# The second MLP product of two token groups as seven block products, with sums of weight and hidden blocks on GpSimd

## The chip, the cores and the metric

One core of one Trainium2 chip. The metric is the device time of one launch in microseconds (us), median of several runs.

## The reference, cut to what matters

One step of a two-layer network over 1152 tokens (128 context tokens and 1024 latent tokens), width 1024, everything in float32. Each layer has a mixer (a short convolution with windowed attention in layer 0, gated linear attention, GLA, in layer 1) and then an MLP with 4096 hidden columns:

```
def sq_relu_mlp(h, w1, w2):
    return jnp.square(jax.nn.relu(h @ w1)) @ w2
...
    x = x + gt1 * rms_norm(mix, norm_g[1])
    h = rms_norm(x, norm_g[2]) * (1 + sc2) + sh2
    x = x + gt2 * rms_norm(sq_relu_mlp(h, w1, w2), norm_g[3])
```

The change is in the last product of that MLP, `(hidden) @ w2`, for 768 of the 1152 tokens, in both layers.

## The kernel before, in words

The 1152 tokens are nine tiles of 128, in three groups of three (`GROUPS`, `GT`; a group is `GN` = 384 tokens). Every float32 product is made as three products of rounded parts: an operand x is split into x_hi, which ScalarE (ACT) writes by a copy to the rounded type, and x_lo = x - x_hi, which VectorE (DVE) writes. The product is hi*hi + hi*lo + lo*hi, three matmuls of TensorE (PE).

The MLP of a layer has three stages on PE.

1. **Group 0**, `mlp_step` and PE's `up` and `down`: for each of 32 hidden rows f the first product (L2545), and with the row before it the second product into the accumulators `acc(0)` to `acc(2)` (L2467), two PSUM banks each, one for every tile of tokens.
2. **Pairs**, `pairs` and PE's `pair_products` (L2580): the first product of groups 1 and 2, for 16 jobs j of two hidden rows each (`JOBS`). A 2x2 block product (two hidden rows by two halves of the inner dimension, times two halves by two groups) is made as seven block products with sums (`PRODUCTS` = 7). A block product is one step: 12 matmuls of 384 columns; a job is 84. DVE makes the weight sums (`sum_weights`, L1925) and the lo parts (`split_piece`, L1932) of job j+1 while PE works at job j, and adds the products (`sum_block`, L1948); its order is written out by hand: step 0 has three weight sums and a split, step 1 has `sum_block` 0 and a split, and so on. PE's step 3 waits for `sum_block` 0, which empties the bank that step 3 writes. ACT applies the ReLU (`relu_block`, L1257), GpSimd (POOL) squares each of the four blocks of a job in place (`square_blocks`, L902), and SyncE (SP) stores them in `hid_scratch` in HBM (`block_out`).
3. **Held rows**: the second product of groups 1 and 2. For group 1 and then group 2 it runs over 32 hidden rows. A row n needs a panel of `mlp_w2` (128x1024, 512 KB) and a stored hidden block (128x384). SP loads both when PE has used the row four before it (`down` and `held_in`, L582 and L720; four slots), ACT rounds both (`round_held`, L1262 and L983), DVE splits both (`split_held`, L1953 and L1601), two rows ahead of PE in their programs, and PE's `rows_panel` (L2467) does 18 matmuls of 512 columns: three tiles, three parts, two halves. After each group `post_square` (ACT) and `post_add` (DVE) read the accumulators, scale them by the norm and add them to `xt`; the first read by DVE frees an accumulator for PE.

Each engine runs its own program in order; semaphores tie them. After layer 0's MLP the first panels of the GLA projection follow (L2649); after layer 1's the output rows are written.

## Time and profile before

| | us |
|---|---|
| median of 3 runs (2780.16 to 2782.31) | 2782.21 |
| the profiled execution, whole | 2780.66 |
| its span, first to last instruction | 2778.9 |
| held rows of layer 1, within the span | 2504.6 to 2768 |
| pairs of layer 0, steady part | 885 to 1098 |

The profile is of one execution. A busy share is busy time over the span. Matmuls overlap in the pipeline, so the time of one is better read from a long run of them divided by their number than from the duration in its row. The time of an instruction of DVE, ACT or POOL runs from when the engine took it up to its end, so it holds any time in which the instruction could not get at its operands.

### The profile page before, as it was taken

How to read it: one execution, taken by the hardware profiler on the slowest of the kernel's cores; microseconds unless marked ns; L12 is line 12 of the kernel's file. 1: busy time of each engine (PE TensorE's matmuls, PEld its weight loads, DVE VectorE, ACT ScalarE, POOL GpSimd, SP SyncE). 2: the span in 40 equal slices, each digit the busy share in tenths (PEclk: the TensorE clock that was granted, in tenths of full speed). 3: DMA queues.
4: the chain of work that ended last, by engine and by line, in shares of the span. 5: the costliest groups of instructions: out<-in, count | busy, mean ns of one | idle time of the engine just before them, and what ended most of it. 6: DMA issues, size and time to landing. Idle time of an engine off the chain costs nothing.

```text
span 2778.9 us, 37923 instructions
## 1 busy us (share of the span) xinstructions
PE 2675.1 (96%) x14835; PEld 2351.4 (85%) x14835; DVE 1608.3 (58%) x2516; ACT 1285.3 (46%) x2216; POOL 312.8 (11%) x308
## 2 busy tenths in 40 slices
PE   5999999999999999999999998889999999999998
PEld 3878888889998999878898886777899989998787
DVE  4246666564567775555522458985645577764444
ACT  5134445554444444444423676764544444443433
POOL 0000000000001222000000007971000002220000
PEclk8999999999999999999999999999999999999999
DMA  7743332633333444554413451025334434436554
GB/s 274 213 152 96 98 98 70 190 119 124 121 122 121 121 127 165 172 192 169 145 46 102 144 167 53 1 70 200 118 121 122 123 113 125 130 124 205 177 191 146
DMA packets 238909, 372.86 MB, mean 134 GB/s; under 512 B 24806, under 2 KB 181932, under 8 KB 237708
## 3 DMA queue, kind: packets, MB, share of 16 engines
q1 hardware_dynamic: 232496, 352.71, 40.0%
q10 hardware_dynamic: 4220, 9.86, 1.0%
q0 software_dynamic: 2016, 7.86, 0.7%
q8 instruction: 119, 1.95, 0.3%
q14 instruction: 58, 0.48, 0.1%
HBM read 329.88 MB, written 40.50 MB: 133 GB/s over the span
## 4 chain that ended last, share of the span: by engine, by line
PE 86%; DVE 5%; ACT 4%; DMA 2%; issue 2%; SPq 1%; POOL 0%; DVEq 0%; ACTq 0%; POOLq 0%
PE ps L2467 39%; PE ps L2580 16%; PE ps L2545 9%; PE ps L2281 8%; PE ps L2649 4%; PE ps L2242 3%; PE ps L2335 2%; PE ps L2362 1%; PE ps L2298 1%; DVE t_g L1790 1%; PE ps L2745 1%; ACT prT L1072 1%; SPq L622 1%; DVE xx L2105 1%; ACT junk_n L1139 1%
## 5 line engine op out<-in xcount | busy, mean ns | idle before, releaser
L1601 DVE TENSOR_TENSOR p_lo<-p_raw,p_hi 128x1024 fp32r<-128x1024 f32 x379 | 465.6, 1231 | 378.9 <-ACT p_hi L983 378.1
L983 ACT ACTIVATE p_hi<-p_raw 128x1024 fp32r<-128x1024 f32 x379 | 397.4, 1051 | 232.4 <-DMA p_raw<-mlp_w 121.7
L902 POOL TENSOR_TENSOR c_out<-c_out 128x384 f32<-128x384 f32 x128 | 117.9, 932 | 1601.7 <-ACT c_out L1257 1601.7
L2467 PE MATMUL ps<-p_hi,hq_hi 128*128 128x512 f32 x768 | 238.7, 392 | 4.8 <-DVE t_g L1790 4.8
L2467 PE MATMUL ps<-p_hi,hq_lo 128*128 128x512 f32 x768 | 236.7, 389 | 0.0
L2467 PE MATMUL ps<-p_lo,hq_hi 128*128 128x512 f32 x768 | 236.6, 389 | 0.0
L1262 ACT ACTIVATE hq_hi<-hq_raw 128x384 fp32r<-128x384 f32 x128 | 67.0, 523 | 268.9 <-DMA hq_raw<-hid_scratch 268.7
L2580 PE MATMUL ps<-t_hi,w_hi 128*128 128x384 f32 x512 | 173.2, 338 | 10.8 <-DVE t_g L1790 7.6
L1953 DVE TENSOR_TENSOR hq_lo<-hq_raw,hq_hi 128x384 fp32r<-128x384 f32 x128 | 71.9, 562 | 187.6 <-ACT hq_hi L1262 187.5
L2580 PE MATMUL ps<-t_lo,w_hi 128*128 128x384 f32 x512 | 172.9, 338 | 0.0
L2580 PE MATMUL ps<-t_hi,w_lo 128*128 128x384 f32 x512 | 172.9, 338 | 0.0
L2467 PEld LDWEIGHTS ps<-p_hi,hq_hi 128*128 128x128 f32 x768 | 142.5, 188 | 35.5 <-DVE t_g L1790 5.6
L2545 PE MATMUL ps<-hm_hi,p_lo 128*128 128x384 f32 x512 | 172.0, 336 | 0.0
L2545 PE MATMUL ps<-hm_hi,p_hi 128*128 128x384 f32 x512 | 171.7, 335 | 0.0
L2545 PE MATMUL ps<-hm_lo,p_hi 128*128 128x384 f32 x512 | 171.5, 335 | 0.0
L2467 PEld LDWEIGHTS ps<-p_lo,hq_hi 128*128 128x128 f32 x768 | 144.2, 188 | 30.3
L2467 PEld LDWEIGHTS ps<-p_hi,hq_lo 128*128 128x128 f32 x768 | 144.2, 188 | 30.1
L2281 PE MATMUL ps<-h_hi,p_hi 128*128 128x384 f32 x432 | 158.8, 368 | 3.9 <-DVE h_lo L1622 3.9
L2281 PE MATMUL ps<-h_hi,p_lo 128*128 128x384 f32 x432 | 145.6, 337 | 0.0
L2281 PE MATMUL ps<-h_lo,p_hi 128*128 128x384 f32 x432 | 145.2, 336 | 0.0
L1932 DVE TENSOR_TENSOR w_lo<-w_pair,w_hi 128x512 fp32r<-128x512 f32 x128 | 104.6, 820 | 49.9 <-ACT w_hi L1236 49.9
L1948 DVE TENSOR_TENSOR c_sum<-ps,c_sum 128x384 f32<-128x384 f32 x160 | 88.8, 555 | 75.3 <-PE ps L2580 71.9
(298 smaller groups left out, 6050.0 us busy)
## 6 DMA issues: line engine op xcount, KB each, us to landing
p_raw<-mlp_w SPq DMA_DIRECT2D x256, 512.0 KB, 3.4
mod_p<-mod_w SPq DMA_DIRECT2D x80, 512.0 KB, 4.2
w_pair<-mlp_w SPq DMA_DIRECT2D x32, 1024.0 KB, 5.8
p_raw<-gla_w_in SPq DMA_DIRECT2D x56, 512.0 KB, 3.6
hid_scratch<-c_out SPq DMA_DIRECT2D x128, 192.0 KB, 1.9
hq_raw<-hid_scratch SPq DMA_DIRECT2D x128, 192.0 KB, 3.4
p_raw<-gla_w_out SPq DMA_DIRECT2D x24, 512.0 KB, 3.4
mod_w<-mod_w SPq DMA_DIRECT2D x8, 1024.0 KB, 19.0
```

Of the source, the lines that this page charges most:

```text
L902: nc.gpsimd.tensor_tensor(c_out[n % 4][:], c_out[n % 4][:], c_out[n % 4][:], ALU.mult).then_inc(c_squared, 1)
L983: nc.scalar.activation(p_hi[s][:, :, 0:width], p_raw[s][:, :, 0:width], ACT.Copy).then_inc(pan_hi, 1)
L1601: V.tensor_tensor(p_lo[s][:, :, 0:width], p_raw[s][:, :, 0:width], p_hi[s][:, :, 0:width].bitcast(F32), ALU.subtract).then_inc(pan_lo, 1)
L1932: V.tensor_tensor(w_lo[layer][i][:], raw_piece(j, step), w_hi[layer][i][:].bitcast(F32), ALU.subtract).then_inc(piece_lo, 1)
L1948: V.tensor_tensor(out[:], b, x[:], ALU.add).then_inc(c_summed, 1)
L1953: V.tensor_tensor(hq_lo[layer][n % 4][:], hq_raw[layer][n % 4][:], hq_hi[layer][n % 4][:].bitcast(F32), ALU.subtract).then_inc(hq_ready, 1)
L2242: return M.transpose(out, in_, ident[0:n, 0:n])
L2281: mm = M.matmul(ps[:, b, 0:GN], w[s][:, c, :], h0[n][x][:, c, :], start=(c == 0 and x == 0 and w is p_hi), stop=(c == DC - 1 and w is p_lo))
L2467: mm = M.matmul(acc(slot)[:, cols], x, flat(w[s])[:, cols], start=begin and edge == 0, stop=end and edge == 2)
L2545: mm = M.matmul(ps[:, b, 0:GN], w[s][:, c, :], x[:, c, :], start=(c == 0 and x is hi and w is p_hi), stop=(c == DC - 1 and w is p_lo))
L2580: mm = M.matmul(ps[:, c_bank(j, which), 0:GN], w[layer][i][:, c, :], second_operand(layer, step, x, c), start=(step < 3 and c == 0 and x = ...
L2649: mm = M.matmul(ps[0:width, b, 0:GN], w[s][:, c, 0:width], hx[g][x][:, c, :], start=(c == 0 and x == 0 and w is p_hi), stop=(c == DC - 1 a ...
```

## The change

The second product of groups 1 and 2 is now also made as seven block products. For each of 16 panel pairs j, the hidden blocks (two groups by two hidden rows) times the weight blocks (two hidden rows by two halves of 512 output columns) are one 2x2 block product. The seven go in four passes, each over all 16 pairs: passes 0, 1 and 3 have two block products for each panel, one in each half of the accumulators (18 matmuls), and pass 2 has one (9 matmuls). So a layer has 64 panels as before, 16 of them with half the matmuls.

- The four sums of hidden blocks (`s1`, `q11`, `s2`, `s4`) are made by POOL after the squares, in `square_blocks`, and seven blocks of a job are stored in place of four (`blocks_out`, `STORED`).
- The sums of weight blocks are made by POOL in `panel_sums`, on 128x512 each: one in pass 0, two in pass 1, one in pass 2. The first is kept in `w_hold` for the later passes. ACT's rounding of such a panel waits for POOL (`pan_summed`).
- Loads of a panel: 512 KB in passes 0, 1 and 3 (in pass 1 as two halves of two panels), 256 KB in pass 2. Loads of hidden blocks: two blocks (384 KB) in passes 0, 1 and 3, one in pass 2.
- Between passes the accumulators are read out: ACT copies them to `pp` after pass 0; DVE makes `second_sums` and `second_rest` after pass 1, `third_sum` after pass 2 (which completes group 1 in `xn`), and `fourth_sum` after pass 3 (which completes group 2 in `pp`). `post_square` and `post_add` of groups 1 and 2 then read `xn` and `pp` in SBUF, no longer PSUM.

The diff, cut to its core:

```diff
+    w_hold = [[at(f"w_hold{l}{j}", [P, CC, P], F32, o + 2048 * j if j < 12 else rest + 2048 * (j - 12)) for j in range(JOBS)]
+              for l, o, rest in ((0, RC, RA + TAIL), (1, RA, RC))]
+    pp = [at(f"pp{l}", [P, GT, D], F32, o + TAIL) for l, o in ((0, RD), (1, RB))]
+    u_sum = at("u_sum", [P, GT, D // 2], F32, RS)
...
+        STORED = ((c_out[1], 5, 1, 2), (c_out[2], 4, 2, 3), (None, 1, 3, 4), (c_out[3], 0, 3, 5), (c_out[0], 3, 0, 6),
+                  (None, 2, 3, 7), (None, 6, 3, 8))
...
+        def held_halves(n):
+
+            return (0, 1) if n // JOBS != 2 else (0,)
+
+        def raw_half(layer, s, n, half):
+
+            kind, j = divmod(n, JOBS)
+            if kind + half == 1 and kind < 2:
+                return w_hold[layer][j][:]
+            return p_raw[s][:, CC * half:CC * (half + 1), :]
...
+                def blocks_out(j):
+
+                    for i, (x, r, k, made) in enumerate(STORED):
+                        if x is None:
+                            x = s_out[layer][{1: 0, 2: 1, 6: 2}[r]]
+                        sp.wait_ge(c_squared, 8 * (JOBS * layer + j) + made)
+                        sp.dma_start(hid_d[j, r], x[:]).then_inc(hid_out[k], 16)
+
+                def rows_in(n):
+
+                    kind, j = divmod(n, JOBS)
+                    s = fed[0] % SLOTS
+                    fed[0] += 1
+                    sp.wait_ge(pan_used, T.next(pan_used))
+                    if kind in (0, 3):
+                        sp.dma_start(p_raw[s][:], w2[2 * j + kind // 3]).then_inc(pan_in[s], 16)
+                    elif kind == 1:
+                        sp.dma_start(p_raw[s][:, 0:CC], w2[2 * j + 1][:, CC:DC]).then_inc(pan_in[s], 16)
+                        sp.dma_start(p_raw[s][:, CC:DC], w2[2 * j][:, CC:DC]).then_inc(pan_in[s], 16)
+                    else:
+                        sp.dma_start(p_raw[s][:, 0:CC], w2[2 * j + 1][:, 0:CC]).then_inc(pan_in[s], 16)
...
+            def panel_sums(layer, n):
+
+                kind, j = divmod(n, JOBS)
+                s, value = panel_landed[layer, n]
+                last_job = PRODUCTS * (JOBS * layer + JOBS - 1)
+                raw = [p_raw[s][:, CC * h:CC * (h + 1), :] for h in range(2)]
+                hold = w_hold[layer][j][:]
+                if n == 0:
+                    pool.wait_ge(product, last_job + 1)
+                    pool.wait_ge(piece_lo, last_job + PRODUCTS)
+                if n == 3:
+                    pool.wait_ge(product, last_job + PRODUCTS)
+                    pool.wait_ge(c_relu, 4 * JOBS * (layer + 1))
+                pool.wait_ge(pan_in[s], value)
+                if kind == 0:
+                    nc.gpsimd.tensor_tensor(hold, raw[1], raw[0], ALU.subtract).then_inc(pan_summed, 1)
+                elif kind == 1:
+                    nc.gpsimd.tensor_tensor(hold, raw[0], hold, ALU.subtract)
+                    nc.gpsimd.tensor_tensor(raw[1], raw[0], raw[1], ALU.subtract).then_inc(pan_summed, 1)
+                else:
+                    nc.gpsimd.tensor_tensor(raw[0], raw[0], hold, ALU.subtract).then_inc(pan_summed, 1)
+
             def square_blocks(layer):
-                for n in range(4 * JOBS):
-                    pool.wait_ge(c_relu, 4 * JOBS * layer + n + 1)
-                    nc.gpsimd.tensor_tensor(c_out[n % 4][:], c_out[n % 4][:], c_out[n % 4][:], ALU.mult).then_inc(c_squared, 1)
+                q11, q22, q21, q12 = (x[:] for x in c_out)
+                s1, s2, s4 = (x[:] for x in s_out[layer])
+                for j in range(JOBS):
+                    n = JOBS * layer + j
+                    if j == JOBS - 1:
+                        panel_sums(layer, 0)
+                    pool.wait_ge(c_relu, 4 * n + 1)
+                    nc.gpsimd.tensor_tensor(q11, q11, q11, ALU.mult).then_inc(c_squared, 1)
+                    pool.wait_ge(c_relu, 4 * n + 2)
+                    nc.gpsimd.tensor_tensor(q22, q22, q22, ALU.mult).then_inc(c_squared, 1)
+                    if j == JOBS - 1:
+                        panel_sums(layer, 1)
+                    pool.wait_ge(c_relu, 4 * n + 3)
+                    nc.gpsimd.tensor_tensor(q21, q21, q21, ALU.mult).then_inc(c_squared, 1)
+                    if n:
+                        pool.wait_ge(hid_out[3], HID_BASE + 64 * n)
+                    pool.wait_ge(c_squared, 8 * n + 3)
+                    nc.gpsimd.tensor_tensor(s1, q11, q21, ALU.add).then_inc(c_squared, 1)
+                    if j == JOBS - 1:
+                        panel_sums(layer, 2)
+                    pool.wait_ge(c_relu, 4 * n + 4)
+                    nc.gpsimd.tensor_tensor(q12, q12, q12, ALU.mult).then_inc(c_squared, 1)
+                    pool.wait_ge(c_squared, 8 * n + 5)
+                    nc.gpsimd.tensor_tensor(q11, q12, q11, ALU.subtract).then_inc(c_squared, 1)
+                    nc.gpsimd.tensor_tensor(s2, s1, q12, ALU.subtract).then_inc(c_squared, 1)
+                    pool.wait_ge(c_squared, 8 * n + 7)
+                    nc.gpsimd.tensor_tensor(s4, q22, s2, ALU.subtract).then_inc(c_squared, 1)
+                for n in range(3, 3 * JOBS):
+                    panel_sums(layer, n)
...
-                    act.wait_ge(hid_out[k], HID_BASE + 16 * n)
+                    act.wait_ge(hid_out[k], HID_BASE + (64 if k == 3 else 16) * n)
+                    act.wait_ge(c_squared, 8 * n)
...
-                act.wait_ge(hq_in[n % 4], HQ_BASE + 16 * (HELD_ROWS // 4 * layer + n // 4 + 1))
-                nc.scalar.activation(hq_hi[layer][n % 4][:], hq_raw[layer][n % 4][:], ACT.Copy).then_inc(hq_rounded, 1)
-                panel_hi()
+                m = len(held_halves(n))
+                act.wait_ge(hq_in[n % 4], HQ_BASE + 16 * (HELD // 4 * layer + n // 4 + 1))
+                nc.scalar.activation(hq_hi[layer][n % 4][:, 0:m], hq_raw[layer][n % 4][:, 0:m], ACT.Copy).then_inc(hq_rounded, 1)
+                if n >= 3 * JOBS:
+                    panel_hi()
+                    return
+                s = split[0] % SLOTS
+                split[0] += 1
+                T.add(pan_in[s], 32 if n // JOBS == 1 else 16)
+                act.wait_ge(pan_summed, 3 * JOBS * layer + n + 1)
+                for half in held_halves(n):
+                    last = nc.scalar.activation(p_hi[s][:, CC * half:CC * (half + 1), :], raw_half(layer, s, n, half), ACT.Copy)
+                last.then_inc(pan_hi, 1)
...
-                for n in range(HELD_ROWS):
-                    f, g = n % NF, n // NF + 1
-                    if g == 2 and f == 0:
+                for t in range(GT):
+                    T.add(acc_done[t], MLP_USES - 1)
+                for n in range(HELD):
+                    if n == JOBS:
                         for t in range(GT):
-                            post_square(layer, 1, 1, t)
-                    if n + 2 < HELD_ROWS:
+                            act.wait_ge(acc_done[t], acc_count(layer, t, 1))
+                            nc.scalar.activation(pp[layer][:, t, :], acc(t), ACT.Copy).then_inc(acc_read[t], 1)
+                    if 3 * JOBS <= n < 3 * JOBS + GT:
+                        post_square(layer, 1, 1, n - 3 * JOBS)
+                    if n + 2 < HELD:
                         round_held(layer, n + 2)
...
+                if part and g:
+                    own(V.scalar_tensor_tensor(out=t_g[:], in0=(None, xn, pp[layer])[g][:, t, :], scalar=r, in1=gate, op0=ALU.mult,
+                                               op1=ALU.mult))
+                    x = xt[layer][:, i, :]
+                    V.tensor_tensor(x, x, t_g[:], ALU.add).then_inc(x_new, 1)
+                    return
...
-                dve.wait_ge(hq_rounded, HELD_ROWS * layer + n + 1)
-                V.tensor_tensor(hq_lo[layer][n % 4][:], hq_raw[layer][n % 4][:], hq_hi[layer][n % 4][:].bitcast(F32),
+                m = len(held_halves(n))
+                dve.wait_ge(hq_rounded, HELD * layer + n + 1)
+                V.tensor_tensor(hq_lo[layer][n % 4][:, 0:m], hq_raw[layer][n % 4][:, 0:m], hq_hi[layer][n % 4][:, 0:m].bitcast(F32),
                                 ALU.subtract).then_inc(hq_ready, 1)
-                panel_lo()
+                if n >= 3 * JOBS:
+                    panel_lo()
+                    return
+                s = split[0] % SLOTS
+                split[0] += 1
+                dve.wait_ge(pan_hi, T.next(pan_hi))
+                for half in held_halves(n):
+                    c = slice(CC * half, CC * (half + 1))
+                    last = V.tensor_tensor(p_lo[s][:, c, :], raw_half(layer, s, n, half), p_hi[s][:, c, :].bitcast(F32), ALU.subtract)
+                last.then_inc(pan_lo, 1)
+
+            def second_sums(layer, t):
+
+                half = D // 2
+                x = acc(t)
+                first = pp[layer][:, t, 0:half]
+                dve.wait_ge(acc_read[t], acc_count(layer, t, 1))
+                dve.wait_ge(acc_done[t], acc_count(layer, t, 2))
+                own(V.tensor_tensor(u_sum[:, t, :], first, x[:, 0:half], ALU.add))
+                V.tensor_tensor(xn[:, t, 0:half], u_sum[:, t, :], x[:, half:D], ALU.add).then_inc(acc_read[t], 1)
+
+            def second_rest(layer, t):
+
+                half = D // 2
+                second = pp[layer][:, t, half:D]
+                dve.wait_ge(acc_read[t], acc_count(layer, t, 2))
+                own(V.tensor_tensor(xn[:, t, half:D], xn[:, t, 0:half], second, ALU.add))
+                own(V.tensor_tensor(second, u_sum[:, t, :], second, ALU.add))
+
+            def third_sum(layer, t):
+
+                x = xn[:, t, 0:D // 2]
+                dve.wait_ge(acc_done[t], acc_count(layer, t, 3))
+                V.tensor_tensor(x, x, acc(t)[:, 0:D // 2], ALU.add).then_inc(acc_read[t], 1)
+
+            def fourth_sum(layer, t):
+
+                x = pp[layer][:, t, :]
+                dve.wait_ge(acc_done[t], acc_count(layer, t, 4))
+                V.tensor_tensor(x, x, acc(t), ALU.add).then_inc(acc_read[t], 1)
+                dve.wait_ge(acc_read[t], acc_count(layer, t, 4))
...
-                for n in range(HELD_ROWS):
-                    f, g = n % NF, n // NF + 1
-                    if g == 2 and f == 0:
+                for t in range(GT):
+                    T.add(acc_read[t], MLP_USES - 1)
+                for n in range(HELD):
+                    if n == 2 * JOBS:
                         for t in range(GT):
-                            post_add(layer, 1, 1, t)
-                    if n + 2 < HELD_ROWS:
+                            second_sums(layer, t)
+                    if 2 * JOBS < n <= 2 * JOBS + GT:
+                        second_rest(layer, n - 2 * JOBS - 1)
+                    if n == 3 * JOBS:
+                        for t in range(GT):
+                            third_sum(layer, t)
+                    if 3 * JOBS <= n < 3 * JOBS + GT:
+                        post_add(layer, 1, 1, n - 3 * JOBS)
+                    if n + 2 < HELD:
                         split_held(layer, n + 2)
...
+                for t in range(GT):
+                    fourth_sum(layer, t)
...
-                    V.scalar_tensor_tensor(out=xn[:, t, c], in0=acc(t)[:, c], scalar=r, in1=gate2[1][:, 1, c], op0=ALU.mult,
+                    V.scalar_tensor_tensor(out=xn[:, t, c], in0=pp[1][:, t, c], scalar=r, in1=gate2[1][:, 1, c], op0=ALU.mult,
...
-                for n in range(HELD_ROWS):
-                    f, g = n % NF, n // NF + 1
+                for n in range(HELD):
+                    j = n % JOBS
                     s = next_panel()
-                    pe.wait_ge(hq_ready, HELD_ROWS * layer + n + 1)
-                    rows_panel(s, lambda x, t: (hq_hi, hq_lo)[x][layer][n % 4][:, t * P:(t + 1) * P], f == 0, f == NF - 1,
-                               order=(2, 0, 1) if n == 0 else (0, 1, 2), before=blocks_taken if n == 0 else None)
-                    if layer == 0 and 8 <= f < 16:
-                        turn_chunk(f % 2, f - 8)
+                    pe.wait_ge(hq_ready, HELD * layer + n + 1)
+                    halves = held_halves(n)
+                    order = (2, 0, 1) if n == 0 else (0, 1, 2)
+                    for t in order:
+                        if j == 0:
+                            pe.wait_ge(acc_read[t], acc_uses[t])
+                            if n == 0:
+                                blocks_taken(t)
+                            acc_uses[t] += 1
+                        for x, w, edge in ((hq_hi, p_hi, 0), (hq_hi, p_lo, 1), (hq_lo, p_hi, 2)):
+                            for half in halves:
+                                cols = slice(512 * half, 512 * (half + 1))
+                                mm = M.matmul(acc(t)[:, cols], x[layer][n % 4][:, half, t * P:(t + 1) * P], flat(w[s])[:, cols],
+                                              start=(j == 0 and edge == 0), stop=(j == JOBS - 1 and edge == 2))
+                                if t == order[0] and edge == 0 and half == 0:
+                                    used_before(mm)
+                        if j == JOBS - 1:
+                            mm.then_inc(acc_done[t], 1)
+                    if j == JOBS - 1:
+                        late[0] += 1
+                    else:
+                        mm.then_inc(pan_used, 1)
...
-    io["hid_scratch"] = nc.dram_tensor("hid_scratch", ((GROUPS - 1) * NF, P, GN), F32, kind="Internal").ap()
+    io["hid_scratch"] = nc.dram_tensor("hid_scratch", (JOBS, PRODUCTS, P, GN), F32, kind="Internal").ap()
```

## Rows read from the trace of the kernel before

**Rows 1.** The page: busy us (share of the span) and instructions of each engine.
```profile
PE 2675.1 (96%) x14835; PEld 2351.4 (85%) x14835; DVE 1608.3 (58%) x2516; ACT 1285.3 (46%) x2216; POOL 312.8 (11%) x308
```

**Rows 2.** Busy time in windows: pairs and held rows.
```profile
core 0: us, PE busy (x) PEld busy (x) DVE busy (x) ACT busy (x) POOL busy (x), PEclk, DMA share, GB/s
885.00:1098.00 213.00, 212.34 (x1225) 212.29 (x1226) 153.43 (x232) 93.62 (x176) 53.77 (x59) 1.00 0.41 127
...
2504.60:2768.00 263.40, 261.05 (x1150) 215.19 (x1149) 118.81 (x136) 97.43 (x138) 3.69 (x5) 1.00 0.54 182
```

**Rows 3.** The chain in order of time: start us, us, what.
```profile
885.66 212.49 PE ps L2580 x1224
...
2504.65 122.46 PE ps L2467 x540
```

**Rows 4.** Waits, held rows of layer 1: us in total, times, longest.
```profile
PE ps L2467 <- DVE t_g L1790: 2.4, 3, 1.0
```

**Rows 5.** POOL's lines by source: duration ns min/median/max, first and last start.
```profile
L902 POOL TENSOR_TENSOR c_out<-c_out x128: 828/828/1808, 874.4 to 2505.9; 128x384 f32<-128x384 f32 x128
...
L868 POOL TENSOR_TENSOR gk<-gk,ek x8: 1266/1286/1293, 1711.5 to 1833.8; 128x512 f32<-128x512 f32 x8
...
L917 POOL TENSOR_TENSOR oo<-o_b,og x9: 2362/2372/3354, 1840.5 to 1882.6; 128x1024 f32<-128x1024 f32 x9
```

**Rows 6.** Timeline, one pair job's start: start us, us, instruction [idle before].
```profile
1025.18 0.83 POOL L902 TENSOR_TENSOR c_out<-c_out 128x384 f32<-128x384 f32 x1 [1.71 <-ACT c_out L1257]
1026.64 1.21 POOL L902 TENSOR_TENSOR c_out<-c_out 128x384 f32<-128x384 f32 x1 [0.63 <-ACT c_out L1257]
...
1025.38 0.56 DVE L1948 TENSOR_TENSOR c_sum<-ps,c_sum 128x384 f32<-128x384 f32 x1 [0.30 <-PE ps L2580]
1025.86 0.70 DVE L1932 TENSOR_TENSOR w_lo<-w_sum,w_hi 128x512 fp32r<-128x512 f32 x1
1026.47 0.68 DVE L1925 TENSOR_TENSOR w_sum<-w_pair 128x512 f32<-128x512 f32 x1
1027.26 1.13 DVE L1925 TENSOR_TENSOR w_sum<-w_sum,w_pair 128x512 f32<-128x512 f32 x1
...
1029.54 0.56 DVE L1948 TENSOR_TENSOR c_sum<-ps,c_sum 128x384 f32<-128x384 f32 x1
```

**Rows 7.** Timeline of POOL and DVE where their instructions meet.
```profile
881.50 1.00 POOL L902 TENSOR_TENSOR c_out<-c_out 128x384 f32<-128x384 f32 x1 [0.23 <-ACT c_out L1257]
...
1845.60 1.90 POOL L921 TENSOR_TENSOR oo<-oo,rs 128x1024 f32<-128x1024 f32 x1 [2.75 <-DVE rs L2164]
1847.45 3.35 POOL L917 TENSOR_TENSOR oo<-o_b,og 128x1024 f32<-128x1024 f32 x1
...
881.73 1.31 DVE L1925 TENSOR_TENSOR w_sum<-w_pair 128x512 f32<-128x512 f32 x1
...
1846.13 2.44 DVE L1601 TENSOR_TENSOR p_lo<-p_raw,p_hi 128x1024 fp32r<-128x1024 f32 x1
```

**Rows 8.** Timeline of one held row: SP's issue, ACT, DVE.
```profile
2521.48 0.43 SPq L720 DMA_DIRECT2D hq_raw<-hid_scratch  x1
...
2524.89 0.53 ACT L1262 ACTIVATE hq_hi<-hq_raw 128x384 fp32r<-128x384 f32 x1 [2.58 <-DMA hq_raw<-hid_scratch]
...
2526.40 1.23 DVE L1601 TENSOR_TENSOR p_lo<-p_raw,p_hi 128x1024 fp32r<-128x1024 f32 x1 [0.39 <-ACT p_hi L983]
```

**Rows 9.** Timeline, end of layer 0's MLP: splits of two GLA panels, and PE.
```profile
1361.42 0.96 DVE L1601 TENSOR_TENSOR p_lo<-p_raw,p_hi 128x768 fp32r<-128x768 f32 x1 [2.58 <-ACT p_hi L983]
...
1375.25 1.22 DVE L1601 TENSOR_TENSOR p_lo<-p_raw,p_hi 128x1024 fp32r<-128x1024 f32 x1
...
1376.73 0.33 PE L2649 MATMUL ps<-hx_hi,p_hi 128*128 128x384 f32 x1
```

**Rows 10.** Timeline, DVE at the end of the kernel: first and last long instruction.
```profile
2768.12 1.28 DVE L2225 SCALAR_TENSOR_TENSOR xn<-ps,st_n,gate 128x1024 f32<-128x1024 f32 x1
...
2774.53 1.20 DVE L2233 TENSOR_TENSOR xt<-xt,xn 128x512 f32<-128x512 f32 x1
```

83 lines of the change are left out of this document (48 added, 35 removed).

## The prediction, as put on record before the changed kernel was run

> **What bounds the kernel now.** I read the page first: PE is busy for 96% of the span, DVE 58%, ACT 46%, POOL 11% [rows 1]. So time is won where PE has less to do, as long as nobody makes it wait instead. Next, the windows [rows 2]. In the pairs PE is busy 212.3 of 213 us, but DVE also 153.4, and POOL 53.8. In the held rows PE is busy 261 of 263.4 us, DVE 119, ACT 97, POOL almost nothing, at 182 GB/s and a DMA share of 0.54. The granted clock is 1.00 in both (2.4 GHz), and nothing here changes what PE does before it. Both stages run at PE's pace. The chain in order of time gives its unit costs [rows 3]: held rows 122.46 / 540 = 0.2268 us a matmul, 4.08 us a row of 18; pairs 212.49 / 1224 = 0.1736, so 2.08 us a step and 14.58 us a job.
>
> **What the change removes.** Per layer 64 x 18 = 1152 matmuls become 16 x (18 + 18 + 9 + 18) = 1008. Twice 144 at 0.2268 is **-65.3 us**. At each change of group PE also waited for `post_add`, 2.4 us a layer [rows 4]. Now ACT copies the accumulators out in pass 0 to 1 (a tile is done 1.36 us before the next, and PE comes back to it 2.7 us after it ended), DVE's `third_sum` is one short instruction, and only `second_sums` (two of about 0.68 a tile, against 0.68 us of PE a tile in pass 2) is late, by some 0.35 us: **-4.1**.
>
> **What POOL's new work costs by itself.** A square of 384 columns takes 0.83 us. For two different inputs there are rows of 512 columns (1.27 to 1.29) and of 1024 (2.36) [rows 5]; on that line 384 columns take 0.99. The bounds are 0.83 and 1.05. A pair job has four such sums more; by POOL's busy time alone (4 x 0.83 + 4 x 0.99 = 7.3 of 14.58 us) they would be hidden.
>
> **But POOL and DVE get in each other's way.** In [rows 7] a DVE split of 1024 columns takes 2.44 us in place of 1.22: it was taken at 1846.13, POOL's L921 ended at 1847.50, and the split ended at 1848.57. POOL's next instruction, taken at 1847.45, then took 3.35 in place of 2.36. Each waited for the other's instruction. At 881.50 POOL's square took 1.00, while the weight sum that DVE took right behind its split, at 881.73, took 1.31 in place of 0.68: POOL, which had asked first, got in between two DVE instructions. `sum_block`, with one input in PSUM, is not slowed: 0.56 beside a POOL square [rows 6]. So they take turns, in order of asking, wherever DVE reads two SBUF tiles. From the two ends: DVE's 1.22 begins at 1847.35, 0.15 before POOL's end, and POOL's 2.36 begins at 1848.44, 0.13 before DVE's. A hand-over overlaps by about 0.14 us.
>
> The Trainium skill states this in SBUF — State Buffer, section Who interferes with whom: a DVE instruction with two SBUF inputs contends with a GpSimd instruction that reads SBUF, and the second one "fully blocks". The trace agrees but for the 0.14 us. Without that overlap the sum below would be that of the rival "no overlap".
>
> **The pair stage.** DVE's order from a job's start in [rows 6]: `sum_block` 4 at 1025.38 (PE started the job at about 1025.33), split, three weight sums, split (the last two lie in the gap of the rows), `sum_block` 0 from 1029.54 to 1030.10. PE needs that at 1025.33 + 3 x 2.08 = 1031.58: 1.5 us of slack. One POOL square lies in that stretch now (q12). After the change s1 comes before it, and the subtractions q11 and s2 behind it, all before DVE is through (s4 is too late to matter). Each pushes DVE back by 0.99 less the two overlaps, plus the 0.08 that DVE's instructions gain on each other anyway: 0.79. Three are 2.4 us, less 1.5 of slack: PE stands **0.9 us** before step 3. In job 0 POOL has nothing left over, in job 15 DVE has no weight sums, so 14 jobs a layer: 28 x 0.9 = **+25**. Bounds: at 0.83 a sum 0.4 us (+11); at the full 0.99 without overlap 1.47 (+41). The rest of the job has room: ACT's new wait for all eight counts of the job before comes at product 5, 10.4 us into the job, where POOL is done by about 8.
>
> **The held rows.** The last job's handover: `round_held`(1) waits for POOL's second panel sum behind two squares, DVE's last `sum_block` stands behind that split, and PE wants it at its second accumulator: 1 us, and as much at panel 3, whose sum is behind eight instructions: 1.5 a layer, **+3** (0 to 8).
>
> A slot is used again three rows later: 12.2 us in passes 0, 1, 3, and 6.1 in pass 2. Now the block is issued at 2521.48, lands at 2524.89, and the row is split at 2527.63 [rows 8]: 6.5 us after its slot was free (SP's panel issue is 0.4 before). In pass 0 this grows by a sum and larger blocks to some 8.3: hidden. In pass 1 turns count: POOL 2 x 1.27, DVE 0.96 for 768 columns [rows 9] and 2 x 0.68, less overlaps about 4.3 of 4.08 us; a lag of 3 us is absorbed first: 1.5 a layer, **+3**. In pass 2 the smaller load (256 and 192 KB) lands a little earlier, the sum lies beside the block's landing, ACT and DVE have half: about 6.5 against 6.1, a period of (6.5 + 2.04) / 4 = 2.13 for 2.04; and `second_rest` puts 4 us of two-input work on DVE in three rows. 4 a layer, **+8** (0 to 22, if the load of 225 GB/s adds 2 us to the chain). Pass 3 has no POOL work; `third_sum` and `post_add` (8 us over three rows) fit before the two rows already made are used up.
>
> **The ends.** In layer 0 DVE splits the first GLA panel at 1361.42; PE takes it two parts of 4.2 us ahead of 1376.73, at about 1368.3, when it is through with the held rows; the second is split by 1376.47, 0.3 us before PE takes it [rows 9]. Behind `fourth_sum`, which waits for PE's last tile, the first comes 1.3 + 1.0 us after PE's end, and the second still 0.9 late: **+3.2** (1 to 5). In layer 1 DVE's last chain (2768.12 to 2775.73 [rows 10]) began 0.8 us before PE ended; now it begins 1.4 after, and scaling from SBUF also takes turns with POOL's add: **+3** (2 to 4).
>
> **Sum.** -65.3 - 4.1 + 25 + 3 + 3 + 8 + 3.2 + 3 = -24. Against the profiled execution (2780.7) 2756.5; the median of the runs is 1.5 above it: **2758**.
>
> **Rivals.**
> - *The sums are hidden.* If POOL's sums cost PE nothing (it is busy half the job), pair stage and held rows lose nothing: -65.3 - 4.1 + 3.2 + 3 = -63: 2719. For it: POOL's busy times. Against: PE's slack of 1.5 us, which three inserted turns use up. It decides if an insertion costs under 0.5 us. Chance 0.2, with all that ends below 2735.
> - *No overlap.* Turns at full length: pairs 28 x 1.47 = 41; pass 1 (2.54 + 2.32 - 4.08) x 32 = 25; pass 2 (1.27 + 1.24 - 2.04) x 32 = 15: 81 in place of 36, so +21: 2803. Slower. It decides where a hand-over overlaps by less than about 0.05 us; the rows say 0.14, but between 1024-column instructions. Chance 0.12.
> - *The same.* The same mechanism half way, or pass 2's chain at 9 us (a period of 2.76, +23): 2777 to 2787. Chance 0.13.
> - *The forecast*, 2735 to 2776: 0.55.
>
> About 0.2% (5.6 us) is what a measurement of this kernel can tell from no change. Faster 0.75, same 0.13, slower 0.12. The range, 2728 to 2789, leaves out the lower half of the first rival and most of the second; the forecast's own is 2740 to 2775.
>
> **What would show it.** Held rows: 1008 matmuls at 0.2268 a layer, passes 0 and 3 at 4.08 us a row. Pairs: a job of 15.5 us, PE idle on `sum_block` before step 3, L1925 and L1932 near 1.2 us where they were 0.68. Pass 2 above 2.04 us a row, with ACT waiting for POOL. A gap of about 2 us before L2649, and a tail 3 us longer. I am wrong if a pair job stays at 14.58, if POOL's sums are not 1 to 1.3 us, or if loads at 225 GB/s land much later than now.

## The result, and the profile after

Slower. The kernel after takes 2842.82 us (median of 4 runs, 2839.15 to 2847.47), the kernel before on the same chip 2782.2: ratio 1.0221, 95% interval 1.0202 to 1.0239, 60.6 us more. The forecast was 2758, 24 us less. The profiled execution took 2839.15 us, its span is 2837.3.

The page of the kernel after, busy us (share of the span) and instructions, as [rows 1]:

```profile
PE 2652.5 (93%) x14547; PEld 2314.8 (82%) x14547; DVE 1827.0 (64%) x2616; ACT 1317.2 (46%) x2286; POOL 680.2 (24%) x564
```

PE has 288 matmuls less and is busy 22.6 us less, in a span that is 58.4 us longer. So it is PE's idle time that grew, and no engine took PE's place as the busiest. Windows cut at the stages (SP's first weight load, first and last matmul of the held rows) show where. Kernel before:

```profile
core 0: us, PE busy (x) PEld busy (x) DVE busy (x) ACT busy (x) POOL busy (x), PEclk, DMA share, GB/s
...
848.50:1098.00 249.50, 243.33 (x1381) 240.95 (x1380) 181.29 (x271) 110.29 (x207) 57.22 (x63) 0.99 0.40 125
1098.00:1368.30 270.30, 267.88 (x1201) 220.49 (x1200) 137.60 (x182) 117.97 (x182) 3.44 (x4) 1.00 0.55 183
...
2253.80:2504.50 250.70, 244.48 (x1381) 242.06 (x1381) 181.04 (x271) 110.33 (x207) 57.15 (x63) 0.99 0.40 124
2504.50:2768.20 263.70, 261.35 (x1151) 215.45 (x1151) 119.08 (x137) 97.63 (x138) 3.79 (x5) 1.00 0.54 182
```

Kernel after:

```profile
848.70:1123.00 274.30, 249.46 (x1382) 243.03 (x1380) 219.43 (x270) 108.17 (x206) 138.24 (x123) 0.98 0.46 149
1123.00:1394.80 271.80, 246.77 (x1056) 196.40 (x1056) 206.62 (x229) 134.66 (x216) 106.20 (x72) 0.97 0.63 200
...
2287.00:2562.30 275.30, 249.25 (x1380) 242.85 (x1378) 219.24 (x270) 108.09 (x206) 137.86 (x123) 0.98 0.46 149
2562.30:2823.40 261.10, 241.61 (x1008) 192.50 (x1008) 186.52 (x185) 115.79 (x174) 106.19 (x73) 0.96 0.63 202
```

| us, both layers | before | after | change | forecast |
|---|---|---|---|---|
| pairs, up to the first held row | 500.2 | 549.6 | +49.4 | +28 |
| held rows | 534.0 | 532.9 | -1.1 | -58 |
| wait at GLA's first panel (layer 0) | 0 | 2.5 | +2.5 | +3.2 |
| tail (layer 1) | 10.7 | 13.9 | +3.2 | +3 |
| all else | | | +4.4 | 0 |
| span | 2778.9 | 2837.3 | +58.4 | -24 |

The whole saving of matmuls is given back in the held rows, and the pairs cost nearly twice the forecast. What ends PE's waits in the held rows of layer 0 and of layer 1, with the wait just before the first row (us in total, times, longest):

```profile
PE ps L2803 <- DVE p_lo L2083: 12.3, 7, 3.4
PE ps L2803 <- DVE xn L2108: 8.1, 1, 8.1
PE ps L2803 <- DVE c_sum L2067: 3.3, 1, 3.3
PE ps L2838 <- DVE p_lo L1714: 2.5, 1, 2.5
PE ps L2803 <- ACT pp L1406: 2.0, 1, 2.0
...
PE ps L2803 <- DVE p_lo L2083: 10.0, 8, 2.5
PE ps L2803 <- DVE xn L2108: 7.5, 1, 7.5
```

L2083 is the split of a panel with POOL's sums, L2108 `third_sum`, L2067 `sum_block`, L1406 ACT's copy of the accumulators into `pp`. By the starts of the matmuls behind them the waits stand at four places: the start of the held rows (9.5 us in layer 0, 6.4 in layer 1), the copy between pass 0 and pass 1 (2.0 and 1.8), three or four rows of pass 2 (5.8 and 5.3), and `third_sum` before pass 3 (8.1 and 7.5).

**A pair job.** From the chain of the kernel after, and the timeline of the same job (POOL's sums are L984 to L993):

```profile
1017.63 8.60 PE ps L2750 x48
...
1033.58 8.57 PE ps L2750 x48
```

```profile
1027.07 1.27 POOL L984 TENSOR_TENSOR s_out<-c_out,c_out 128x384 f32<-128x384 f32 x1
1027.39 1.50 DVE L2044 TENSOR_TENSOR w_sum<-w_pair 128x512 f32<-128x512 f32 x1
...
1029.65 1.35 POOL L990 TENSOR_TENSOR c_out<-c_out,c_out 128x384 f32<-128x384 f32 x1
1030.05 1.51 DVE L2044 TENSOR_TENSOR w_pair<-w_pair 128x512 f32<-128x512 f32 x1
...
1030.97 1.45 POOL L991 TENSOR_TENSOR s_out<-s_out,c_out 128x384 f32<-128x384 f32 x1
1031.47 1.50 DVE L2051 TENSOR_TENSOR w_lo<-w_pair,w_hi 128x512 fp32r<-128x512 f32 x1
...
1032.89 0.54 DVE L2067 TENSOR_TENSOR c_sum<-ps,c_sum 128x384 f32<-128x384 f32 x1
...
1033.58 0.41 PE L2750 MATMUL ps<-t_hi,w_hi 128*128 128x384 f32 x1 [1.12 <-DVE c_sum L2067]
```

Each of the three DVE instructions waits for one of POOL's sums: 1.50 us in place of 0.68. PE stands 1.12 us for `sum_block` 0, queued behind them. A job takes 15.95 us (1017.63 to 1033.58), 15.93 over several, where it took 14.57.

**Job 1.** The first job in which POOL has sums left over is dearer. DVE has the last reading of group 0's accumulators ahead of it, so PE already waited there in the kernel before, for 1.5 us:

```profile
885.66 0.41 PE L2580 MATMUL ps<-t_hi,w_hi 128*128 128x384 f32 x1 [1.50 <-DVE c_sum L1948]
```

In the kernel after it is 3.7 us (3.9 in layer 1), and the granted clock around the wait's end is at its lower level, 1.2 GHz (the second view is of windows):

```profile
887.52 0.66 PE L2750 MATMUL ps<-t_hi,w_hi 128*128 128x384 f32 x1 [3.73 <-DVE c_sum L2067]
```

```profile
886.40:893.40 7.00, 5.88 (x19) 5.91 (x20) 4.77 (x8) 1.12 (x3) 1.33 (x1) 0.51 0.66 206
```

By the starts of PE's matmuls, the pairs' +49.4 is 38.1 for 28 jobs at 1.36, some 6 more in job 1 of both layers, and 5.4 just before the first row of both.

**The start of the held rows.** SP (issues), POOL and PE in the kernel after:

```profile
1112.25 0.32 SPq L743 DMA_DIRECT2D hid_scratch<-s_out  x1
...
1114.02 1.99 SPq L769 DMA_DIRECT2D hq_raw<-hid_scratch  x4
...
1122.99 0.74 PE L2803 MATMUL ps<-p_hi,hq_hi 128*128 128x512 f32 x2 [2.55 <-DVE p_lo L2083]
...
1129.34 1.19 PE L2803 MATMUL ps<-p_hi,hq_hi 128*128 128x512 f32 x2 [3.29 <-DVE c_sum L2067]
...
1135.25 1.61 POOL L993 TENSOR_TENSOR s_out<-c_out,s_out 128x384 f32<-128x384 f32 x1
...
1136.82 1.29 POOL L959 TENSOR_TENSOR w_hold<-p_raw 128x512 f32<-128x512 f32 x1
1137.25 0.43 SPq L752 DMA_DIRECT2D p_raw<-mlp_w  x1
```

SP's queue gives out the last store of job 14 before the first loads of hidden blocks (1114.02), and the stores of job 15 before row 4's panel (1137.25); POOL's queue has all of job 15's block sums before the panel sum of row 3 (1136.82). PE stands for the last `sum_block` in the middle of row 0, before its third accumulator (1129.34), and later for the rows.

**Between pass 0 and pass 1.** One more instruction that frees accumulators stands behind work for the rows to come. ACT in the kernel after:

```profile
1203.14 2.85 ACT L1406 ACTIVATE pp<-ps 128x1024 f32<-128x1024 f32 x3
```

PE made the last matmul of pass 0 just before 1202 and stands until 1204.31, 2.0 us. ACT's program has the rounding of row 17 ahead of the copy, and in layer 0 also the reading of a piece of group 0 that PE transposes behind row 15. In layer 0 the wait is 2.0 us in every version below, with POOL's panel sums or without them; in layer 1 it is 1.5 to 2.1 with them, 0.9 (e5) and 0.8 (e11) without.

**Between pass 2 and pass 3.** POOL, SP, ACT, DVE and PE in the kernel after:

```profile
1311.04 0.93 POOL L1000 DMA_DIRECT2D x_scratch<-xt  x1
...
1311.35 0.44 SPq L769 DMA_DIRECT2D hq_raw<-hid_scratch  x1
...
1319.38 0.84 ACT L1362 ACTIVATE hq_hi<-hq_raw 128x768 fp32r<-128x768 f32 x1 [3.47 <-DMA hq_raw<-hid_scratch]
...
1322.34 1.88 DVE L2108 TENSOR_TENSOR xn<-xn,ps 128x512 f32<-128x512 f32 x3
...
1323.17 1.19 PE L2803 MATMUL ps<-p_hi,hq_hi 128*128 128x512 f32 x2 [8.15 <-DVE xn L2108]
```

The block of row 49, issued at 1311.35, lands at 1319.38: 8.0 us, where the median of such loads in this kernel is 4.5. DVE splits row 49 first, then does `third_sum`, and only that frees the accumulator that the first row of pass 3, long ready, writes. And one line stands where the prediction did not look for it: POOL's store of 1.5 MB of `xt`, at 1311.04. In the kernel before POOL issued it here:

```profile
1100.21 0.93 POOL L907 DMA_DIRECT2D x_scratch<-xt  x1
```

**The clock.** Windows around that wait, kernel after:

```profile
1310.00:1320.00 10.00, 5.02 (x23) 3.82 (x21) 3.58 (x4) 3.57 (x5) 1.97 (x2) 1.00 0.90 322
1320.00:1330.00 10.00, 6.83 (x23) 5.53 (x24) 9.29 (x12) 7.13 (x12) 0.00 (x0) 0.66 0.54 197
```

The clock falls to the 1.2 GHz level at about 1320, while PE stands, and so is 0.66 over the second ten us; two matmuls take 1.05 us (1324.16) where they take 0.62 from 1327.22 on, at 2.4 GHz again.

### The profile page after: what moved, and what is told of

Read it like the earlier page. It is cut to its first block, busy times and chain, and to the rows that moved or that the text cites. A ratio compares the mean times of both kernels' runs of the same rounds, so it can differ in the third digit from the quotient of the medians.

```text
span 2837.3 us, 37896 instructions
## 1 busy us (share of the span) xinstructions
PE 2652.5 (93%) x14547; PEld 2314.8 (82%) x14547; DVE 1827.0 (64%) x2616; ACT 1317.2 (46%) x2286; POOL 680.2 (24%) x564
## 4 chain that ended last, share of the span: by engine, by line
PE 70%; DVE 13%; ACT 5%; DMA 5%; issue 3%; POOL 3%; SPq 1%; DVEq 0%; ACTq 0%; POOLq 0%
PE ps L2637 20%; PE ps L2803 10%; PE ps L2715 9%; PE ps L2750 9%; PE ps L2451 8%; PE ps L2838 4%; DVE w_lo L2051 3%; PE ps L2412 2%; DVE w_sum L2044 2%; DMA hq_raw<-hid_scratch 2%; DVE w_pair L2044 2%; PE ps L2505 1%; PE ps L2532 1%; DMA p_raw<-mlp_w 1%; PE ps L2934 1%
## 5 line engine op out<-in xcount | busy, mean ns | idle before, releaser
L1714 DVE TENSOR_TENSOR p_lo<-p_raw,p_hi 128x1024 fp32r<-128x1024 f32 x283 | 347.8, 1232 | 334.7 <-ACT p_hi L1076 333.7
L1076 ACT ACTIVATE p_hi<-p_raw 128x1024 fp32r<-128x1024 f32 x283 | 296.9, 1052 | 223.7 <-DMA p_raw<-mlp_w 117.5
L974 POOL TENSOR_TENSOR c_out<-c_out 128x384 f32<-128x384 f32 x32 | 27.5, 860 | 1414.5 <-ACT c_out L1356 1414.5
L2803 PE MATMUL ps<-p_hi,hq_lo 128*128 128x512 f32 x672 | 220.0, 397 | 0.0
L2803 PE MATMUL ps<-p_lo,hq_hi 128*128 128x512 f32 x672 | 220.0, 397 | 0.0
L2803 PEld LDWEIGHTS ps<-p_hi,hq_hi 128*128 128x128 f32 x672 | 126.1, 193 | 90.8 <-DVE p_lo L2083 35.6
L2073 DVE TENSOR_TENSOR hq_lo<-hq_raw,hq_hi 128x768 fp32r<-128x768 f32 (+1 forms) x128 | 133.5, 1043 | 100.4 <-ACT hq_hi L1362 100.1
L1362 ACT ACTIVATE hq_hi<-hq_raw 128x768 fp32r<-128x768 f32 (+1 forms) x128 | 97.8, 764 | 182.9 <-DMA hq_raw<-hid_scratch 182.5
L2051 DVE TENSOR_TENSOR w_lo<-w_pair,w_hi 128x512 fp32r<-128x512 f32 x128 | 127.6, 999 | 50.6 <-ACT w_hi L1334 50.6
L2750 PEld LDWEIGHTS ps<-t_hi,w_hi 128*128 128x128 f32 x512 | 98.5, 192 | 54.0 <-DVE w_lo L2051 45.8
## 6 DMA issues: line engine op xcount, KB each, us to landing
p_raw<-mlp_w SPq DMA_DIRECT2D x96, 256.0 KB, 3.4
```

Source lines behind the costliest of these rows:

```text
L1076: nc.scalar.activation(p_hi[s][:, :, 0:width], p_raw[s][:, :, 0:width], ACT.Copy).then_inc(pan_hi, 1)
L1362: nc.scalar.activation(hq_hi[layer][n % 4][:, 0:m], hq_raw[layer][n % 4][:, 0:m], ACT.Copy).then_inc(hq_rounded, 1)
L1714: V.tensor_tensor(p_lo[s][:, :, 0:width], p_raw[s][:, :, 0:width], p_hi[s][:, :, 0:width].bitcast(F32), ALU.subtract).then_inc(pan_lo, 1)
L2051: V.tensor_tensor(w_lo[layer][i][:], raw_piece(j, step), w_hi[layer][i][:].bitcast(F32), ALU.subtract).then_inc(piece_lo, 1)
L2073: V.tensor_tensor(hq_lo[layer][n % 4][:, 0:m], hq_raw[layer][n % 4][:, 0:m], hq_hi[layer][n % 4][:, 0:m].bitcast(F32), ALU.subtract).then_ ...
L2750: mm = M.matmul(ps[:, c_bank(j, which), 0:GN], w[layer][i][:, c, :], second_operand(layer, step, x, c), start=(step < 3 and c == 0 and x = ...
```

## The experiments

A time without a ratio is of one execution; the kernel before, run beside each of them, took 2781.8 to 2783.5 (medians). Executions of one kernel lie up to 8 us apart, and up to 10 in e12, so small differences are read from a stage or a wait and not from the time. "Pairs" is from the first weight load to the first held row; the two numbers are layers 0 and 1 (after: 274.3 and 275.3). "Held rows" is from there to the first matmuls of the last tile (after: 270.5 and 259.7).

**e1: POOL's sums of hidden blocks left out** (the sums become a memset or one column, the counts stay):

```diff
-nc.gpsimd.tensor_tensor(s1, q11, q21, ALU.add)
+nc.gpsimd.memset(s1, 0.0)
```

> Leaves out: the four sums of hidden blocks (three are a memset of POOL, which reads nothing, one is a single column); the stores and waits stay. Theory A (POOL's sums and DVE's two-input instructions take turns ahead of sum_block 0): a pair job falls from 15.93 to 14.6 us, 14 jobs a layer, 38 us for both layers, so about 2802 where the changed kernel has 2839 to 2847. Rival (the seven stores in place of four, or ACT's new wait for POOL's counts, hold the job up): the job stays at 15.9 and the time above 2835.

2789.93 us, span 2788.1, 12 less than expected. Pairs 251.3 and 250.5, the job 14.56. So 47.8 of the +49.4 come with these four instructions a job, and not only the 38 of the turns: the wait in job 1 is back at 1.5 us in both layers, and in layer 0 its slow matmuls are gone. The wait before row 0 stays, at 2.2 and 1.6 us. For the held rows the cut changed little (270.0 and 255.5).

**e2: `sum_block` 0 ahead of step 0's split**, behind the weight sums:

```diff
                                 for i in range(3):
                                     sum_weights(layer, j + 1, i)
+                                sum_block(layer, j, 0)
```

> Nothing left out: DVE makes sum_block 0 before the split of step 0, not behind it. Theory A, place of the stall (sum_block 0 is late because it stands behind everything that took turns): it comes 1.4 us earlier, so a job falls from 15.93 to 14.6 or 14.7 us and the time by 35, to about 2807. Rival (the shared access is full over the whole job, 14 us of turns in 14.6): the job stays above 15.5, and the time above 2830.

2805.73, span 2803.9, pairs 257.7 and 256.5. All sums are still made, and a steady job costs PE nothing. The price of the turns was paid only since one late instruction stood behind them in a queue. In layer 0 the pairs' remaining +8.2 has waits in jobs 1 and 2 (2.3 and 0.7 us) and before row 0 (3.2). Timeline of this kernel at the same place in a job:

```profile
1020.84 1.50 DVE L2044 TENSOR_TENSOR w_pair<-w_pair 128x512 f32<-128x512 f32 x1
...
1022.27 0.55 DVE L2067 TENSOR_TENSOR c_sum<-ps,c_sum 128x384 f32<-128x384 f32 x1
1022.73 1.03 DVE L2051 TENSOR_TENSOR w_lo<-w_pair,w_hi 128x512 fp32r<-128x512 f32 x1
```

The turn of the third weight sum is as long as before; `sum_block` now stands ahead of the split, the last of them, which takes 1.03 us here.

**e3: SP's loads between its stores** (the blocks of rows 0 and 1 before the rest of job 14's stores, rows 4 to 6 between those of job 15):

```diff
-                    blocks_out(j)
+                    blocks_out(j, 0, PRODUCTS if j < JOBS - 2 else 4)
```

> Nothing left out: SP issues the loads of held rows 0 to 6 between the stores of the last two pair jobs, not behind them. Theory B (the loads stand behind stores that wait for POOL's last sums): row 4's load is issued about 4 us after the last product in place of 17, row 0 is ready before the last product ends, and from there to the end of pass 0 PE gains 10 to 15 us a layer: about 2818. Rival (POOL's own queue, the panel sum of row 3 behind the last job's squares and sums, is the limit): row 3 stays where it is and the gain is under 4 us a layer: 2835.

2831.72, span 2829.9, 7.4 less, pairs 272.1 and 272.9. The rival was right: row 4's load went out at 1130.57, 6.7 us earlier, but POOL's panel sums of rows 3 and 4 still ran at 1135.10.

**e4: `third_sum` ahead of the split of row 49:**

```diff
-                    if n == 3 * JOBS:
+                    if n == 3 * JOBS - 1:
                         for t in range(GT):
                             third_sum(layer, t)
```

> Nothing left out: DVE makes third_sum before the split of row 49, not behind it. Theory C (PE's 8 us wait at the start of pass 3 is for third_sum, which stands behind a split that waits for row 49's load): pass 3 starts 5 us earlier a layer and PE then waits 0 to 2 us for row 49: 6 to 10 us in all, about 2834. Rival (the loads of rows 48 to 51 come too slowly in any order): the wait only moves to row 49, and the gain is under 2 us in all.

2827.25, span 2825.5. The wait fell from 8.1 to 2.6 us in layer 0 and from 7.5 to 1.6 in layer 1, where PE then waits 2.7 us for row 49. The held rows fell to 265.7 and 254.7.

**e5: POOL's sums of panel halves left out** (memset, or one column of a block):

```diff
-nc.gpsimd.tensor_tensor(hold, raw[1], raw[0], ALU.subtract)
+nc.gpsimd.memset(hold, 0.0)
```

> Leaves out: POOL's sums of weight blocks (in pass 0 a memset, which reads nothing, in passes 1 and 2 a single column of each). Loads, rounding, splits and orders are those of the changed kernel. If turns of POOL and DVE are what makes a row of passes 1 and 2 late, pass 1 runs at 4.08 us a row where it ran at 4.27, and PE's waits for p_lo in pass 2 (about 8 us a layer) shrink to 3 or less: 10 to 16 us in all, about 2830. If the loads are the limit, pass 2 keeps its waits and the gain is under 6 us. The wait at the start of pass 3 (8 us) stays by both, for it is of loads and of DVE's order.

2807.63, span 2805.8: 31.5 us less, twice what was expected. Held rows 256.0 and 246.2, 14 us shorter in each layer, though the wait for `third_sum` is longer there (10.0 and 9.9). For L2083 PE still waits 4.0 and 2.8 us, nearly all of it before the first row (3.2 and 2.6). By the starts of the rows pass 1 takes 65.4 us in both layers (67.9 and 69.1 in the kernel after), which is 4.08 us a row.

**e6: e2, e3 and e4 together.**

> Nothing left out: sum_block 0 ahead of the split, SP's loads between the stores, third_sum ahead of the split of row 49, all three. Alone they brought 33, 7 and 12 us of span. If they are three separate places, the span is 2837 - 52 = 2785; if one stands for another, above 2795.

2786.05, span 2784.3, 53.0 us less than the kernel after. The three add up.

**e7: e6, and the handover:** POOL makes row 3's panel sum ahead of job 15's last two block sums, and ACT and DVE take row 1 behind the last ReLU and `sum_block`.

```diff
+                    if j == JOBS - 1:
+                        panel_sums(layer, 3)
                     nc.gpsimd.tensor_tensor(s2, s1, q12, ALU.subtract).then_inc(c_squared, 1)
...
-                        elif step in (3, 5):
-                            split_held(layer, step // 2 - 1)
+                        elif step in (3, 6):
+                            split_held(layer, step // 3 - 1)
```

> Nothing left out: the three orders, and at the last pair job POOL makes the panel sum of row 3 ahead of its last two hidden sums, and ACT and DVE take row 1 behind the last ReLU and the last sum_block, not ahead of them. Theory B2 (the start of the held rows is bounded by POOL's queue and by sum_block 4 behind a split that waits for POOL): PE's waits of 3.3 us at row 0 and of 3 us and more at row 3 go, 5 to 8 us a layer below the three orders: about 2775. Rival (the loads at 300 GB/s are the limit there): under 2 us a layer.

2778.96, span 2777.2. At the start of the held rows of layer 0 four waits of 0.2 to 0.4 us and one of 2.2 are left.

**e8: e7, and `second_rest` out of the rows of pass 2** (to just before row 48's split):

```diff
-                    if 2 * JOBS < n <= 2 * JOBS + GT:
-                        second_rest(layer, n - 2 * JOBS - 1)
+                    if n == 3 * JOBS - 2:
+                        for t in range(GT):
+                            second_rest(layer, t)
```

> Nothing left out: as the one before, and second_rest (six instructions of two SBUF inputs) is made before the split of row 48, when POOL has no more work, in place of rows 33 to 35. If second_rest and the turns it takes make pass 2 late, PE's two waits of 2 us behind it go, 4 us a layer and 8 in all, and DVE has room for it before row 48, whose load is late anyway: about 2767. If the slot's chain of load, sum, rounding and split is the limit of pass 2, the waits move on, and the gain is under 2 us in all.

2769.47, span 2767.7: held rows 257.5 and 246.7, from 259.7 and 252.1.

**e9: e8, with the half of `second_rest` that only `fourth_sum` needs moved into pass 3, and GLA's first split ahead of `fourth_sum`.**

```diff
-                own(V.tensor_tensor(second, u_sum[:, t, :], second, ALU.add))
...
+                    if 3 * JOBS + 3 <= n < 3 * JOBS + 6:
+                        second_last(layer, n - 3 * JOBS - 3)
...
+                if layer == 0:
+                    panel_lo(width=3 * ZR)
                 for t in range(GT):
                     fourth_sum(layer, t)
```

> The kernel with all the moves so far (second_rest ahead of row 48's split), and two moves more: DVE splits GLA's first panel ahead of fourth_sum (layer 0), and the three instructions of second_rest that only fourth_sum needs go from the rows before pass 3 to rows 51 to 53. In the last kernel DVE's 4.3 us of second_rest ended just as row 48 could be split, PE waited 4.5 us for third_sum in each layer, and 2.5 and 0.4 us for GLA's panels. Theory (DVE's order sets both): the waits before pass 3 fall by 2.1 us a layer, those at GLA go: the span falls from 2767.7 by 4.2 + 2.9 to about 2760.6, the time to about 2762, 0.7% below the kernel before. Rival (the loads of rows 48 to 51, 896 KB each asked for at the pace of pass 2, set the wait before pass 3): only GLA's 2.9 us go, about 2766.

2772.61 (7 runs, 2769.74 to 2776.13), ratio 0.9967 (0.9956 to 0.9979). Both theories were right in part, and the gain did not come. Waits of this kernel, layer 0:

```profile
PE ps L2854 <- DVE p_lo L1721: 3.0, 1, 3.0
PE ps L2819 <- DVE p_lo L1721: 2.7, 1, 2.7
...
PE ps L2819 <- DVE xn L2119: 1.7, 1, 1.7
```

The wait for `third_sum` fell from 4.5 to 1.7, and the next row then waited 2.7 for its block, which had taken 9.9 us to land (issued at 1279.42). GLA's first panel was in time, its second was 3.0 late. Two waits were moved, not removed.

**e11: e8 without POOL's sums of panel halves**, as e5.

> The kernel with second_rest ahead of row 48's split, but POOL's sums of panel halves are left out (its instructions stay, cut to a memset or to one column of each block). On the kernel after, the same cut took 31.5 us. Theory (most of the 31.5 us was the order of work around these sums, and the moves have taken it back; what is left are turns with DVE in passes 1 and 2 and at the start of the held rows, where PE still waits some 10 us in all for p_lo and 2 us for the copies): the span falls from 2767.7 by 6 to 12 us, to about 2758. Rival (the 31.5 us are the price of the instructions themselves, wherever they stand): about 2736.

2748.3, span 2746.5: 21.2 us less than e8, between the two. Held rows 246.4 and 238.7 (11.1 and 8.0 less), pairs 1.1 us less in total. So of the 31.5 us of e5 a third was order; the rest is the price of the sums where they stand, more than PE's named waits for them (6.5 and 3.8 in e8). Part of what has no name is short: pairs of matmuls that start 0.24 to 0.35 us apart in place of 0.227 are 167 in e8's held rows and 85 in e11's, which makes some 5 us.

**e13: the kernel after, with POOL's store of group 0 behind job 7's sums.**

```diff
                     nc.gpsimd.tensor_tensor(s4, q22, s2, ALU.subtract).then_inc(c_squared, 1)
+                    if j == 7:
+                        store_rows(layer, 0)
```

> The kernel after with one move: POOL issues the store of group 0's 1.5 MB of x (x_scratch in layer 0, the outputs in layer 1) behind job 7's sums of blocks, where before it stood behind all panel sums. In the kernel before, POOL reached it at 1100.21; in the kernel after only at 1311.04, in the middle of the loads of rows 48 to 51, where the queue of POOL moved 1.57 MB beside SP's loads and the block of row 49 took 8.0 us to land. Theory (the store takes bandwidth from those loads and is part of the wait before pass 3): that block lands in 6 us or less, PE's waits for third_sum (8.1 and 7.5 us) shrink to 5 to 6.5 each, the kernel gains 3 to 6 us on 2839. Rival (SP's own loads, 896 KB for each 2 us of PE, fill the queue by themselves): the block still takes 7.5 to 8 us, no gain.

2837.57, span 2835.8. The block of row 49 landed in 6.0 us (1312.58 to 1318.60), and the waits for `third_sum` are 2.0 and 2.3 shorter, as the theory has it:

```profile
PE ps L2811 <- DVE xn L2116: 6.1, 1, 6.1
...
PE ps L2811 <- DVE xn L2116: 5.2, 1, 5.2
```

The gain in time is not to be told from the spread of runs: the held rows are 1.2 and 4.2 shorter, and the pairs, where the store now is, 2.3 and 1.3 longer. In the job behind the store PE's wait for `sum_block` 0 is 2.3 and 2.4 us in place of 1.1.

**e12: e9, the early store, and GLA's second split ahead of the last `post_add`.**

```diff
-            for t in range(GT):
+            for t in range(GT - 1):
                 post_add(0, 1, 2, t)
             panel_lo()
+            post_add(0, 1, 2, GT - 1)
```

> All moves so far (the kernel with two more moves, median 2772.6), the early store, and one more: DVE splits GLA's second panel ahead of the last post_add, since with the first panel's split moved PE went into GLA without a wait, and then waited 3.0 us for the second panel. There the waits at the start of pass 3 were 1.7 us for third_sum and 2.7 us for row 49 in layer 0, whose block took 9.9 us to land, 2.7 and 1.0 in layer 1. Theory (the store is what slows these loads): row 49's wait goes, third_sum's stays at 1.7 or less, GLA's 3.0 goes: 3.0 + 2.7 + 1 to 2 = 7 us less, about 2766, 0.6% below before. Rival (the loads alone fill the queue): only GLA's 3.0, about 2769.5.

2767.05 (5 runs, 2763.67 to 2774.12), ratio 0.995 (0.9936 to 0.9963): 0.5% faster than the kernel before, the best version here. Its stages:

```profile
849.70:1104.80 255.10, 245.62 (x1380) 242.60 (x1379) 216.95 (x270) 108.11 (x207) 138.83 (x125) 0.99 0.51 164
1104.80:1360.00 255.20, 243.84 (x1060) 194.22 (x1059) 207.24 (x229) 134.47 (x215) 108.63 (x70) 0.99 0.67 209
...
2249.20:2506.40 257.20, 247.03 (x1382) 243.95 (x1381) 216.64 (x270) 108.38 (x207) 140.29 (x126) 0.98 0.50 164
2506.40:2750.70 244.30, 235.31 (x1009) 186.98 (x1007) 188.52 (x184) 115.48 (x173) 106.77 (x70) 1.00 0.68 211
```

GLA's 3.0 and row 49's 2.7 us are gone (0.3 and nothing in their place), `third_sum` has 2.8 and 2.0. The median is near the theory's 2766, but these runs lie 10 us apart; it is the waits that speak for it. Against the kernel before the held rows are 34.5 us shorter, and the pairs 12.1 longer. Some of that is the early store's own price. POOL issues it at 993.74, SP a load of 1 MB of weights at 994.19, and DVE stands for that load until 1005.28, 11 us later, where the median of such loads in the kernel after is 5.7:

```profile
1005.28 1.00 DVE L2059 TENSOR_TENSOR w_sum<-w_pair 128x512 f32<-128x512 f32 x1 [3.26 <-DMA w_pair<-mlp_w]
```

PE waits 1.9 us there (1008.92), and 2.2 in layer 1.

## Why the prediction was wrong

Right were the matmuls' number and place, the mechanism of turns in the pairs, and both ends. Wrong was what hung on a queue's order: the steps that failed are the start of the held rows (+3), the two readings of accumulators that were put at nothing (`third_sum`, and ACT's copy in the term of -4.1), and, by size, the terms of the pairs (+25) and of passes 1 and 2 (+11). No term stood for the clock. In us: the pairs are 21 over their forecast and the held rows 57. Of these 57 some 33 are waits that PE's rows name (44.5 in place of the 11.7 that the forecast left), and 14 is PE's work at the lower clock.

**The pair stage: mechanism right, the term mis-sized.** Forecast 0.9 us a job, measured 1.36. An insertion costs DVE 0.82 us (1.50 for 0.68) where 0.79 was worked out, and PE's idle is 1.12. The idle is counted from the end of the matmul before, which started at 1032.13; at PE's pace the next was due 0.17 later, so 1033.58 is 1.28 late, and the one behind it comes 0.08 late as well (1033.84). 28 x 1.36 = 38 in place of 25. The slack of 1.5 us was read from a steady job and is not there in job 1, where PE waited in the kernel before already: some 6 us more, half of it or more the clock. The overlap of a hand-over is real (the sum at 1027.07 ends at 1028.34, and DVE's 0.68 us begin at 1028.21), so the rival "no overlap" (1.47 a job) is out, though its total was the nearer. e1 and e2 show the mechanism, and e2 that it is not a bandwidth that is lost: the same sums cost a steady job nothing once `sum_block` 0 stands ahead of the fourth insertion. The Trainium skill's rule (SBUF — State Buffer, Who interferes with whom: the second of two such instructions is blocked fully) holds for each of these turns, but for the overlap at the hand-over.

**The start of the held rows: the step that failed first.** "PE wants it at its second accumulator: 1 us, and as much at panel 3", **+3** (0 to 8). Measured: in layer 0 9.5 us of waits (2.6 before row 0, 3.3 for `c_sum`, at the third accumulator and not the second, 3.6 in two waits up to 1148.5), in layer 1 6.4: 16 in place of 3. Named was what stands behind POOL's panel sums; left out were SP's queue, where seven stores stand in place of four between the last loads, each waiting for a sum, and that in POOL's last job most sums are turns (up to 1.6 us each, eight ahead of row 3). e3, the change of SP's order alone, shortened the pairs by 2 us a layer. e2, e3, e4 and e7 together took 60 us from the kernel after without leaving out any work.

**Pass 3: the claim that failed.** "`third_sum` and `post_add` ... fit before the two rows already made are used up". Rows made ahead are no cover for an instruction that frees the accumulator they write: 8.1 and 7.5 us, forecast 0. e4 took 5.5 and 5.9 of it away. The rest had two causes behind it, the landing of the loads (e9, e13) and the work ahead of them in DVE's queue (e9 against e8). It was the same with ACT's copy after pass 0, in the term of -4.1: PE comes back 2.7 us after a tile ended, and that was to cover a copy of 1 us. But ACT reached it late, behind the rounding of row 17 and more: 2.0 and 1.8 us, forecast 0. No run moved it.

**The loads.** The first rows of pass 3 are asked for at pass 2's pace, with blocks and panels of pass 3's size: in the kernel after SP issues the panels of rows 48 to 50 at 1308.83, 1310.97 and 1313.02, 896 KB a row with the blocks, beside POOL's store. The moved bytes of e8 in 40 slices from 1270 to 1300:

```profile
GB/s 182 217 212 225 240 139 174 265 152 20 30 186 330 137 158 328 382 326 176 206 159 346 421 415 406 425 425 419 409 399 430 399 380 219 64 27 82 175 401 373
```

Eleven slices in a row (8.2 us) stand at 380 to 430, and no slice above. That the loads of that stretch wait for each other is read from this and from the landing times; no run spaced them out. That "loads at 225 GB/s land much later than now" was among what would make the prediction wrong, but it was looked for in pass 2 and not at its end. That POOL's store would slide from 1100 to 1311, behind the panel sums of 45 rows in its queue, was not seen at all.

**Passes 1 and 2: again the size.** Forecast 11 us with POOL's sums. By the starts of the rows, the kernel after against e5: pass 1 is 6 us longer in both layers together, and pass 2, without the wait for `third_sum`, 16: 22 us, twice the forecast. PE's waits for panels there are 11; the rest are delays too short to be listed, and the clock. (Pass 0 gained some 10 us more in e5, and the wait for `third_sum` lost 4.) `second_rest` on DVE in the middle of pass 2 is part of it: e8 gained 7.5 us in the held rows by moving it.

**The clock.** The sum took PE's idle time as the only cost. In layer 1's held rows 1008 matmuls at 0.2268 are 228.6 us; they took 261.1, of which 19.5 are idle. The other 13 are matmuls that took longer or began late. The clock of 0.96 in that stage makes at most 10 (0.04 x 261); PE is busy for 15 of the 20.5 us at the lower level, so it is 7.6. In layer 0's held rows it is some 7. In e12 the clock of layer 1's is 1.00, and the stage is busy for 235.3 us in place of 241.6. The long waits cost more than their own length.

**What stays open.** The +4.4 us outside the changed stages are within the spread of runs; they lie between GLA's start and layer 1's pairs (1394.8 to 2287), where PE is busy for 854.4 us with the matmuls that took 848.5, at a clock of 0.99 for 1.00. Half of e11's gain shows in no wait that PE's rows name; the short delays make some 5 us of it, and the clock of the held rows about 1 (PE is busy at the lower level for 13.1 us in e8's, for 10.7 in e11's). Why they are there was not tried, nor an order in which ACT copies the accumulators first, nor slower loads at the start of pass 3.

## What to carry to other kernels

Give work to an idle engine only with its queues read to the end: what stood behind the new instructions before (here a store of 1.5 MB), and what stands behind the instructions that they slow. A slack is to be read at the worst job and not at a steady one. A wait for a turn cost a steady job nothing once the urgent instruction stood ahead of it (e2); moves in the hand-written orders alone (e2 to e12) turned +2.2% into -0.5% with the same work. Where a stage frees accumulators for the next, the freeing instruction goes ahead of everything that only prepares rows. That a short pass should not ask for the long pass's loads at its own pace is likely from the landing times, and untested.

## What the runs showed of the hardware

A wait of PE of 8 us was followed by about 3.5 us of matmuls at the 1.2 GHz level (1323.17 to 1326.7), one of 2.7 us (e9, up to 1292.49) by such matmuls as well, from about 1293.8 to 1297, and one of 1.7 us (e9, up to 1285.49) by none. The length of the wait alone does not decide: one of 2.0 us was followed by a granted clock of 0.59 over 4.2 us in e1 (from 1176.8) and by 1.00 over ten us in the kernel after (from 1204). POOL's memset and its sums of one column (e1) do not slow DVE: the job is back at 14.56 us. A block of 384 KB lands in 4.5 us as a median; row 49's took 8.0 (kernel after, 322 GB/s over ten us) and 9.9 (e9) beside a store, and 6.0 without the store (e13). A load of 1 MB took 11 us beside the same store (e12), with a median of 5.7 in the kernel after.
